# Half-swaps for the rotary embedding on ScalarE, and reordered entries of conv and attention, in a two-stack transformer kernel

## What is computed

```python
def qkv_heads(z, q_gain, k_gain):
    q = rms_norm(z[..., :Q_END].reshape(z.shape[:-1] + (N_HEADS, HEAD_DIM)), q_gain)
    k, v = kv_heads(z[..., Q_END:V_END], k_gain)
    return q, k, v

def apply_rope(t, cos, sin):
    b, n, h, _ = t.shape
    tf = t.astype(jnp.float32).reshape(b, n, h, 2, 2, ROPE_PAIRS)
    t1, t2 = tf[..., 0, :], tf[..., 1, :]
    c = cos[None, :, None]
    s = sin[None, :, None]
    out = jnp.stack([t1 * c - t2 * s, t1 * s + t2 * c], axis=-2)
    return out.reshape(t.shape).astype(t.dtype)

# first_block, layer l
zl = hl @ w_in[l] + b_in[l]
q_l, k_l, v_l = qkv_heads(zl, q_gain[l], k_gain[l])
q_l = apply_rope(q_l, cos, sin)
k_l = apply_rope(k_l, cos, sin)
attn_l = latent_attention(q_l, k_l, v_l, k_c, v_c)
```

## Time and profile before

| | |
|---|---|
| median of 3 runs | 3144.55 us (3144.37 to 3147.13) |
| the profiled execution's own time | 3145.95 us |
| its span in the trace | 3144.2 us |
| mean granted TensorE clock | 0.995 of full speed |
| busy share of the span | PE 97%, PEld 83%, DVE 63%, ACT 37%, POOL 26% |
| read from HBM | 266.75 MB, 87 GB/s over the span |

### The profile page before, as it was taken

The page is one execution under the profiler, slowest core; times in us unless marked ns, Lnnn a source line. Parts: engine busy times, 40 slices in busy tenths (PEclk is TensorE's granted clock), DMA queues, the critical chain, the costliest instruction groups (busy, mean ns, idle before and its releaser), DMA issues.

```text
span 3144.2 us, 43692 instructions
## 1 busy us (share of the span) xinstructions
PE 3064.6 (97%) x16056; PEld 2598.6 (83%) x16056; DVE 1979.9 (63%) x2784; ACT 1152.7 (37%) x1661; POOL 806.7 (26%) x330
## 2 busy tenths in 40 slices
PE   7999999999999999999999999999999999999998
PEld 5999887899999999997777677778887686777766
DVE  5899987644576164356989985664646466445443
ACT  3122364233243221224334535443223535443443
POOL 0001212233323232231012024511545332233312
PEclk8999999999999999999999999999999999999999
DMA  7442001112212212123541022423233212122212
GB/s 289 175 171 82 28 1 65 45 59 101 81 61 67 73 60 67 61 67 136 193 163 55 1 67 87 144 80 101 94 95 108 75 59 79 54 78 77 78 60 67
DMA packets 77709, 275.25 MB, mean 88 GB/s; under 512 B 8688, under 2 KB 11888, under 8 KB 76656
## 3 DMA queue, kind: packets, MB, share of 16 engines
q1 hardware_dynamic: 70800, 253.94, 24.3%
q10 hardware_dynamic: 6752, 19.14, 1.7%
HBM read 266.75 MB, written 6.29 MB: 87 GB/s over the span
## 4 chain that ended last, share of the span: by engine, by line
PE 89%; DVE 5%; ACT 2%; issue 1%; DVEq 1%; DMA 0%; SPq 0%; ACTq 0%
PE ps L684 53%; PE ps L1065 11%; PE ps L619 5%; PE ps L633 2%; PE ps L800 2%; PE ps L1210 1%; PE ps L872 1%; PE ps L963 1%; PE ps L788 1%; PE ps L993 1%; PE ps L1289 1%; DVE small L2362 1%; PE ps L691 1%; PE ps L1307 1%; PE ps L1016 1%
## 5 line engine op out<-in xcount | busy, mean ns | idle before, releaser
L550 POOL TENSOR_TENSOR w_lo<-w_raw,w_hi 128x1024 fp32r<-128x1024 f32 x308 | 789.8, 2568 | 2195.9 <-ACT w_hi L1398 2195.9
L1398 ACT ACTIVATE w_hi<-w_raw 128x1024 fp32r<-128x1024 f32 x376 | 395.8, 1056 | 561.5 <-PE ps L684 286.6
L684 PE MATMUL ps<-act_hi,w_hi 128*128 128x384 f32 (+1 forms) x2544 | 529.8, 356 | 4.4 <-DVE w_lo L2188 2.5
L684 PE MATMUL ps<-act_hi,w_lo 128*128 128x384 f32 (+1 forms) x2544 | 519.4, 352 | 0.0
L684 PE MATMUL ps<-act_lo,w_hi 128*128 128x384 f32 (+1 forms) x2544 | 519.2, 352 | 0.0
L684 PEld LDWEIGHTS ps<-act_hi,w_hi 128*128 128x128 f32 x2544 | 451.0, 188 | 70.5 <-issue 34.7
L684 PEld LDWEIGHTS ps<-act_hi,w_lo 128*128 128x128 f32 x2544 | 455.0, 188 | 32.4
L684 PEld LDWEIGHTS ps<-act_lo,w_hi 128*128 128x128 f32 x2544 | 454.3, 188 | 32.3 <-issue 0.5
L2256 DVE SCALAR_TENSOR_TENSOR x<-ps,mod,x 128x384 f32<-128x384 f32 (+1 forms) x128 | 64.2, 546 | 277.3 <-PE ps L684 222.7
L2419 DVE SCALAR_TENSOR_TENSOR x<-arena,vec,x 128x512 f32<-128x512 f32 x336 | 228.2, 706 | 0.0
L2411 DVE SCALAR_TENSOR_TENSOR arena<-arena,vec 128x783 f32<-128x783 f32 (+1 forms) x240 | 226.2, 943 | 0.0
(11 more groups left out here) (380 smaller groups left out, 4551.8 us busy)
## 6 DMA issues: line engine op xcount, KB each, us to landing
w_raw<-in_weights SPq DMA_DIRECT2D x376, 512.0 KB, 3.4
arena<-in_ada_w SPq DMA_DIRECT2D x75, 512.0 KB, 4.8
tmp<-in_ada_w SPq DMA_DIRECT2D x21, 512.0 KB, 6.3
x<-in_x SPq DMA_DIRECT2D x2, 1536.0 KB, 19.2
x<-in_x ACTq DMA_DIRECT2D x1, 3072.0 KB, 10.5
arena<-in_pool_w ACTq DMA_DIRECT2D x2, 1024.0 KB, 4.8
x_mid<-x ACTq DMA_DIRECT2D x1, 2048.0 KB, 7.1
x<-x_mid ACTq DMA_DIRECT2D x1, 2048.0 KB, 8.4
```

The source lines that it names most:

```text
L550: nc.gpsimd.tensor_tensor(WL[:, w], raw, WH[:, w].bitcast(f32), ALU.subtract).then_inc(units_split, 1)
L684: last = nc.tensor.matmul(tile(o, o + b - a), w[:, s * UNIT + k * P:s * UNIT + (k + 1) * P], act[:, k * TOK + a:k * TOK + b], start=(n == ...
L1398: nc.scalar.activation(WH[:, s * UNIT:(s + 1) * UNIT], RAW[:, (s % 2) * UNIT:(s % 2 + 1) * UNIT], ACT.Copy).then_inc(hi_done, 1)
```

## The change

It has six parts.

1. ScalarE makes the exchanged halves: behind the writing of head j it copies each half of the partitions to the other half of `T2`, as two 64x512 copies. From j=2 on it first waits for the norm of head j-2 (`norm_done`), which read the same `T2`. VectorE waits for the copies (`swapped`) and multiplies once by the sines, over 128 partitions. The sign in the sine table changes sides.
2. The table load for the exponential moves ahead of the evacuation of V.
3. In layer 1 the refills of slots 2 and 3 move from before the attention into its tiles 4 and 8.
4. One convolution tap runs before the attention's first tile; tiles 0 and 1 have none, tile 2 has one. In layer 1 that is 60 taps in attention for 64 before, and the table's last entry (taps at the first unit of gate2) goes from 12 to 16. In layer 0 it is 31 for 32.
5. In layer 1 the evacuation of the early projection moves from behind the conv's first unit to behind its fourth.
6. In layer 1 the conditioning steps 24 to 31 stand before units 5, 7, 9, 11, 13, 15, 16, 17 of conv and gate0; before, at 3, 5, ..., 17.

GpSimd's and SP's own orders do not change.

```diff
-           (9, 7, 8, (2, 2, 2, 2, 2, 2, 1, 1, 0, 0), 2, (2, 2, 2, 2), 12))
+           (9, 7, 8, (2, 2, 2, 2, 2, 2, 1, 1, 0, 0), 2, (2, 2, 2, 2), 16))
...
-          {**{2 * i + 3: (24 + i,) for i in range(CH)}, **{u: (14 + u,) for u in range(18, 24)}, 24: (38, 39)})
+          {**{u: (24 + i,) for i, u in enumerate((5, 7, 9, 11, 13, 15, 16, 17))}, **{u: (14 + u,) for u in range(18, 24)}, 24: (38, 39)})
...
                     refill(l, "conv", i, s)
-                    if l and u == 0:
+                    if l and u == SLOTS - 1:
                         act.wait_ge(ple_mm, 3)
                         for t, a, n in ((3, 0, 1024), (2, 1024, 512)):
                             nc.scalar.activation(PP_EARLY[:, a:a + n], ps(t, 0, n), ACT.Copy).then_inc(tile_free[t], 1)
...
                     nc.scalar.activation(like_product(AR[:, dst:dst + w], w), product(t, w), ACT.Identity, bias=at(BG, c, 1), scale=v1(l, gain)).then_inc(tile_free[t], 1)
+                    if j > 1:
+                        act.wait_ge(*at_least(l, "norm_done", j - 2 + 1 + 2))
+                    act.drain()
+                    mid = P // 2
+                    for here, there in ((slice(0, mid), slice(mid, P)), (slice(mid, P), slice(0, mid))):
+                        last = nc.scalar.activation(AR[there, T2 + t * SEQ:T2 + (t + 1) * SEQ], AR[here, dst:dst + SEQ], ACT.Copy)
+                    last.then_inc(on(l, "swapped"), 1)
                     if j < 2 * SLOTS or l not in HALVED:
                         refill(l, "qkv", j // SLOTS, j % SLOTS)
...
+                nc.scalar.preload_act_table_set("natural_log_exp_and_others")
                 for s, n in enumerate((1024, 512)):
...
-                if l not in HALVED:
-                    for s in (2, 3):
-                        refill(l, "qkv", 2, s)
-
...
-                nc.scalar.preload_act_table_set("natural_log_exp_and_others")
+                def next_weights(it):
+                    if it in (4, 8):
+                        refill(l, "qkv", 2, 1 + it // 4)
+
                 act.drain()
-                heads("attn", 0, 4, 6, next_query if l in HALVED else None)
+                heads("attn", 0, 4, 6, next_query if l in HALVED else next_weights)
...
                 maximum(0)
                 maximum(1)
+                if also:
+                    also(2)
                 for it in range(n):
...
-                    for here, there in ((slice(0, mid), slice(mid, P)), (slice(mid, P), slice(0, mid))):
-                        V.tensor_tensor(AR[there, T2 + (j % 2) * SEQ:T2 + (j % 2 + 1) * SEQ], AR[here, src:src + SEQ],
-                                        AR[here, SIN:SIN + SEQ], ALU.mult)
+                    dve.wait_ge(*at_least(l, "swapped", j + 1))
+                    V.tensor_tensor(t2, t2, AR[:, SIN:SIN + SEQ], ALU.mult)
                     dve.drain()
...
-                    done = conv_taps(l, done, per_tile[it % 4])
+                    done = conv_taps(l, done, per_tile[it % 4] if it > 2 else int(it == 2))
...
-    sign = np.where(np.arange(P) < P // 2, 1.0, -1.0).astype(f)[:, None]
+    sign = np.where(np.arange(P) < P // 2, -1.0, 1.0).astype(f)[:, None]
```

4 lines of the change are left out of this document (2 added, 2 removed).

## The result

The changed kernel takes 3153.03 us in the median of 11 runs (3151.39 to 3155.65), the kernel before 3146.13 us in 11 runs beside it (3144.03 to 3149.56). The ratio is 1.0025, with a 95% interval of 1.0017 to 1.0033: slower by 5 to 10 us. The prediction was 3149.2 us in a range of 3139.5 to 3156.0. The direction held, and the size was forecast too small: +4.6 us, where the medians differ by 6.9 us and the ratio gives 7.9. The measured median lies 3.8 us above the predicted one; 1.6 us of that are that the kernel before itself took longer here than in the three runs from which the forecast started (3146.13 for 3144.55).

The account below looks back on a forecast made before the run. TensorE (PE), busy 97% of the span, was taken to set the pace, so only its waits count. Terms -1.0 + 3.5 + 2.1 + 0 + 0 = +4.6 us gave a median of 3149.2 us, range 3139.5 to 3156.

Parts of the forecast that it names:

- three waits: PE waits at layer 1's conv start and both layers' attention starts, 8 us together, said to be all the change can reach.
- Layer 0, -1.0 us: Copies hidden in the heads; the 1.01 us PE wait at attention's start goes: -1.0 us (-1.1 to 0).
- Conv, +3.5 us: Layer 1 conv start: unit 5 starts 2.5 us later behind step 24, which costs 1.0 us in the open.
- the clock term: Layer 1 conv start: a new 3.0 us stall may bring a second clock fall; counted 0, +1.7 us in the range.
- The extra step at unit 16: Layer 1 conv: step 24, formerly run in a gap where PE waited anyway, now costs 1.0 us in the open.
- the load for unit 7: Layer 1 conv: it lands at 1489.7, evacuations behind its refill end at 1492.2, and step 24 waits for them.
- Heads, +2.1 us: Layer 1 heads: head 3's copies wait for head 1's norm, holding refill and next square; one +2.1 us delay (0 to 3.3).
- VectorE's saving is worth nothing: Layer 1 heads: VectorE saves 0.69 us per head, but PE does not wait for it.
- Attention, 0: Layer 1 attention start: 3.6 us of waits won, 3.6 us lost to moved refills; together 0 (-3.6 to +1).
- the return: Layer 1 attention: refills moved into tiles 4 and 8 let GpSimd block VectorE, 1.8 us each, +3.6 us.
- gate2, 0 to +1: Layer 1 gate2: four more taps, 2.66 us, make VectorE 2.1 us late against about 2.7 us of slack; 0 to +1.
- the second fall of the clock: Rival: +1.7 us on the sum, and again if the stall ahead of unit 5 exceeds 3 us: 3151 to 3154; chance 0.18.

Follow-up runs that it names:

- c1: Kernel before with only part 2, part 5 and steps 24 to 31 before units 6, 7, 9, 11, 13, 15, 16, 17: 3146.25 us, ratio 1.0004.
- a2: The change with conditioning step 24 one unit later, before unit 6 instead of 5, nothing else: 3148.55 us, ratio 1.0010.
- b1: The change with ScalarE's copies placed behind the refill and the key's root in each head: 3150.86 us, ratio 1.0020.
- c4: The change itself profiled once more, no edit, one execution: 3156.26 us.
- a3: The change with part 1 undone, so VectorE again multiplies by the sines in two operations: 3151.23 us, ratio 1.0020.
- a4: The change with part 3 undone, slots 2 and 3 refilled ahead of attention: 3155.87 us (6 runs), ratio 1.0031.
- c2: Kernel before with part 2 alone, the table load ahead of V: 3144.24 us, ratio 0.9999.
- b3: Kernel before with part 4 alone, the moved convolution taps: 3146.59 us, ratio 1.0003.
- c3: Kernel before with part 1 alone, profiled once more without edit, one execution: 3152.73 us.

## Why the prediction was right or wrong

**Reading and direction.** That PE's path decides, and that time is won or lost only in its waits, held but for the clock: PE's busy time changed by 0.2 us, and the touched stages sum to the measured difference. The prediction speaks of three waits that the change can reach and lists four; a fifth, the 1.46 us at 1708.28, it did not see.

**Layer 0, -1.0 us: wrong, 0.0.** The copies in the heads are hidden, as said. At the attention's start the wait of 1.01 us went, but PE gained only 0.5 us there, since a wait of 1.15 us for GpSimd's low halves of the queries stands nearby in its place. The rest was given back in two steps of 0.4 us: PE waits 0.52 us at 412.40 where it had no wait, and 1.14 us where it waited 0.76 at the start of the context's attention.

**Conv, +3.5 us: mechanism right, size short by the clock.** The step that was mis-sized is the clock term, which I counted as 0 and bounded by 1.7 us; it was 2.4 us. The lower clock of the earlier trace rows had come behind a wait of 2.45 us; it now came behind one of 4.60 us, in step 24 (1.94 us for 1.06, 0.9 us) and in unit 5 (1.5 us).

The other terms, with the 1.35 us added by which the profiled execution was ahead until conv: PE's wait ended at 1491.6, forecast 1492.2, and unit 5 started at 1493.4, forecast 1493.2, which is +2.7 us where +2.5 was forecast. So that term came out nearly right by two errors that cancel, the wait's end 0.6 us early and the step 0.9 us slow. The extra step at unit 16 cost 1.2 us (predicted 1.0). In sum 2.7 for the start of unit 5, 1.5 for its slow matmuls and 1.2 make 5.4 of the 5.5 us.

The wait's end was early because unit 4 started 1.2 us earlier and not 0.6. Unit 4 follows a chain on VectorE from its memset (L2507). In all fourteen traces the memset begins 6.94 to 6.98 us after VectorE's work before it, and in the traces with part 1 that work lies 0.5 us earlier against PE than in those without. In c1, without part 1, unit 4 starts at 1481.74, where the forecast had 1481.83. Why part 1 moves VectorE there stays open. The profile puts the end of the memset's wait down to ScalarE's L1593 in the change, but before, the memset began ahead of that evacuation (1479.28 and 1479.71), so it does not need it.

The wait was 4.60 us and not the 3.0 forecast, because unit 4 started early and ran at full clock. That the end hung on the load for unit 7 and the evacuation behind it was right. And one number of the table made all of it, a2 shows.

**Heads, +2.1 us: right in kind, one head off.** The loop between copies and norms stalls PE once and then no more, as forecast. But it was head 2's copies waiting for head 0's norm, not head 3's for head 1's, and what PE missed was not the emptied product but the key's root behind them, which the profile names as the end of the wait (L1636) and which b1, with refill and root ahead of the copies, bears out. Measured 2.5 us of wait. What I left out again is the clock behind it: in five of the seven traces with this wait PE then lost 1.4 to 2.9 us, and in two nothing. The trace of the change itself is one of the two; its second trace (c4) lost 1.4 us. A copy pair costs 1.27 us (forecast 1.15).

**VectorE's saving is worth nothing: right in layer 1** (a3), open in layer 0's attention.

**Attention, 0: -1.2 us.** The gains were larger than forecast, -5.3 us to the fourth tile in place of -3.6, and the return was 4.2 us, in place of 3.6. The difference in the gains is the wait of 1.46 us that the prediction did not see: 1.3 us of the wait of 2.45 and the whole of the 2.29 went, as counted, and this one too. So the sum is near the forecast because two terms were short, not because both were right. With the refills ahead of attention (a4) the gain is 3.4 us and the return 1.6. So the moved refills gained 2.0 us at the start and gave back 2.6 in tiles 4 and 8, 1.3 each and not 1.8; and the other 1.6 of the return is the work of the next channel, which stood in the start before and now comes later. I had not counted that. The table load counted as 1.3 us in my sum; alone it gives 0.0 (c2). I had counted GpSimd's hold on VectorE for the refills and did not apply it to the operation behind the exponential.

The rule of the Trainium skill ("SBUF — State Buffer", "Who interferes with whom"), that VectorE's and GpSimd's shared ports go to whoever issues first, for the whole instruction, agrees with c2 as far as this: a normalization issued 2.3 us after GpSimd began took 2.81 us, 0.62 without. It ended only behind the second of GpSimd's two operations, and which of the two engines issued first at the change from one to the other the trace does not tell. The 2.66 us that the Trainium skill states for a switch of tables ("ScalarE: Activation LUTs", "What ACT_TABLE_LOAD costs") find no support here: the exponential moved by 1.49 us, and PE gained nothing.

**gate2, 0 to +1: +0.7 us.** The conv's last product came 4.2 us late against PE (1925.16 - 5.65 - 1915.34, the starts of L2434 here and L2425 before) where the slack was 2.7, and PE waited for it:

```profile
1925.16 0.69 DVE L2434 TENSOR_TENSOR x<-x,arena 128x512 f32<-128x512 f32 x1
...
1925.91 1.07 PE L699 MATMUL ps<-x,ones_in_one_column 128*32 128x512 f32 x8 [0.47 <-DVE x L2434]
```

Inside the bound.

**The chances.** The case that came is the forecast with the second fall of the clock added (3151 to 3154), at which I had put 0.18. By the prediction's own line of 0.2% it counts as slower, which had 0.30, and not as no change, which had 0.60. The rows had one wait of 2.45 us with a fall behind it and one without, and I went by the second. That was one observation: the same wait of 2.45 us is followed by a fall in b3 and c3, and its neighbour of 2.29 us in c1.

## What to carry to other kernels

On an engine that is busy without a gap, an edit is priced by where it puts a wait, not by the work it saves: one entry of an order table (a2) and the copies placed behind the refill and the root (b1) removed 7.1 and 2.7 us, while 0.69 us less of VectorE in each of layer 1's ten heads gave none. When an instruction that waits for another engine is added to a queue, list what stands behind it up to the next thing TensorE needs, and put those first. After bringing one operation forward, look at the next engine's first operation: if it now falls where a neighbour holds it up, as GpSimd did VectorE in c2, the gain ends there. And price a wait with the clock that may fall behind it: where the clock fell, the heads' wait of 2.5 us cost 4.1 to 5.6.

## What the runs showed of the hardware

A wait of TensorE of about 2.3 to 2.9 us may or may not be followed by a stretch at half clock (1.2 in place of 2.4 GHz), and this differs between executions of one program: behind the same 2.50 us in the heads the change lost nothing in one trace and 1.4 us in another. Behind all five waits ahead of step 24 (2.79 to 4.60 us) the clock fell, and twice in layer 0 it fell in an attention whose waits were 1.4 us and shorter (b1, c4). A fall cost 1.4 to 2.9 us in the heads, so the wait of 2.5 us cost up to 2.2 times its length. What decides it these runs do not show; they had no kernel that gave TensorE other work during such a wait.
